# Two-block transformer layer stack on one core: in the RWKV pairs, the last accumulator's scaling, the output gate's product and the rounding of the output change places

## The reference, cut to what matters

```python
r, k, v, wd, ad, gd = _split(z, RWKV_SIZES)
decay = jnp.exp(-jnp.exp(w_log)); a = jax.nn.sigmoid(a0 + ad @ a2)
g = jax.nn.sigmoid(gd) @ g2                      # the output gate
def step(S, inp):                                # a scan over 512 tokens
    Sa = einsum('bhvk,bhk->bhv', S, a_t)
    S = S * w_t + Sa * b_t + v_t * k_t
    return S, einsum('bhvk,bhk->bhv', S, r_t)
y = (y - mu) * rsqrt(var + RWKV_LN_EPS) * lnx_g + lnx_b
y = (y + bonus) * g                              # -> y @ w_rwkv_o
```

## Time and profile before

| | us |
|---|---|
| runs shown | 2666.18, 2668.07, 2661.59; median 2666.18 |
| the profiled execution, its own time | 2665.71 |
| its span, first to last instruction | 2663.9 |
| granted TensorE clock, mean | 0.994 of full speed |
| PE busy | 2592.7 (97% of the span) |
| DVE busy | 1457.7 (55%) |
| ACT busy | 632.8 (24%) |
| POOL busy | 1485.9 (56%) |

### The profile page before, as it was taken

The page is one execution under the profiler, slowest core; times in us unless marked ns, Lnnn a source line. Parts: engine busy times, 40 slices in busy tenths (PEclk is TensorE's granted clock), DMA queues, the critical chain, the costliest instruction groups (busy, mean ns, idle before and its releaser), DMA issues.

```text
span 2663.9 us, 47379 instructions
## 1 busy us (share of the span) xinstructions
PE 2592.7 (97%) x16370; PEld 2024.5 (76%) x16370; DVE 1457.7 (55%) x2041; ACT 632.8 (24%) x1159; POOL 1485.9 (56%) x945
## 2 busy tenths in 40 slices
PE   7889999998999999999999999999999999999999
PEld 5667888876776677777888887776677777888887
DVE  7886646364566647774442424557647764443434
ACT  3332000023234414431200002234423431200002
POOL 4466666655544544556666666554444456666665
PEclk9999999999999999999999999999999999999999
DMA  4213233323211122223333333311122223233322
GB/s 152 68 44 103 88 95 93 95 84 103 87 57 50 42 93 60 78 71 97 92 95 94 95 95 108 96 57 42 50 85 68 76 72 100 90 95 94 95 94 95
DMA packets 72725, 222.67 MB, mean 84 GB/s; under 512 B 9344, under 2 KB 12544, under 8 KB 72576
## 3 DMA queue, kind: packets, MB, share of 16 engines
q1 hardware_dynamic: 72576, 220.63, 27.1%
HBM read 218.50 MB, written 2.10 MB: 83 GB/s over the span
## 4 chain that ended last, share of the span: by engine, by line
PE 89%; DVE 5%; DVEq 3%; issue 1%; DMA 1%; POOL 1%; ACT 0%; SPq 0%; ACTq 0%; POOLq 0%
PE acc L479 78%; PE bank L479 10%; DMA raw<-in_w_pg 1%; POOL w_lo L358 0%; PE bank L1057 0%; DVE z L1095 0%; DVEq L1538 0%; DVE rw_bon L1095 0%; DVEq L1275 0%; DVEq L1631 0%; DVE rw_SCB L1095 0%; DVE z_rw L1095 0%; DVE att L1293 0%; DVEq L1294 0%; DVEq L1286 0%
## 5 line engine op out<-in xcount | busy, mean ns | idle before, releaser
L358 POOL TENSOR_TENSOR w_lo<-raw,w_hi 128x1024 fp32r<-128x1024 f32 (+3 forms) x438 | 964.0, 2201 | 298.8 <-PE acc L479 277.9
L351 POOL TENSOR_SCALAR w_hi<-raw 128x1024 fp32r<-128x1024 f32 (+3 forms) x438 | 431.5, 985 | 689.2 <-PE acc L479 585.1
L479 PE MATMUL acc<-xg_hi,w_hi 128*128 128x512 f32 x2224 | 594.9, 404 | 26.8 <-POOL w_lo L358 12.6
L479 PE MATMUL acc<-xg_hi,w_lo 128*128 128x512 f32 x2224 | 587.7, 399 | 0.0
L479 PE MATMUL acc<-xg_lo,w_hi 128*128 128x512 f32 x2224 | 585.7, 399 | 0.0
L479 PEld LDWEIGHTS acc<-xg_hi,w_hi 128*128 128x128 f32 x2224 | 412.3, 189 | 145.8 <-issue 52.3
L479 PEld LDWEIGHTS acc<-xg_lo,w_hi 128*128 128x128 f32 x2224 | 416.9, 189 | 103.7 <-issue 4.8
L479 PEld LDWEIGHTS acc<-xg_hi,w_lo 128*128 128x128 f32 x2224 | 415.0, 188 | 100.0
L1095 DVE TENSOR_TENSOR x<-x,acc 128x512 f32<-128x512 f32 x104 | 71.4, 688 | 322.3 <-PE acc L479 322.0
L1910 ACT ACTIVATE ffn_act<-ffn_t 128x512 f32<-128x512 f32 x100 | 63.3, 633 | 775.7 <-DVEq L1155 619.5
L479 PE MATMUL acc<-hid_hi,w_hi 128*128 128x512 f32 x656 | 182.8, 396 | 3.8 <-POOL w_lo L358 1.6
(11 more groups left out here) (339 smaller groups left out, 2795.1 us busy)
## 6 DMA issues: line engine op xcount, KB each, us to landing
raw<-in_w_up SPq DMA_DIRECT2D x132, 512.0 KB, 3.6
raw<-in_w_down SPq DMA_DIRECT2D x48, 512.0 KB, 3.6
raw<-in_w_gate SPq DMA_DIRECT2D x48, 512.0 KB, 3.6
raw<-in_w_ret SPq DMA_DIRECT2D x32, 512.0 KB, 3.6
raw<-in_w_rw SPq DMA_DIRECT2D x28, 512.0 KB, 3.6
raw<-in_w_o SPq DMA_DIRECT2D x48, 256.0 KB, 2.6
raw<-in_w_in SPq DMA_DIRECT2D x18, 512.0 KB, 3.7
raw<-in_w_down SPq DMA_DIRECT2D x24, 384.0 KB, 3.0
```

The source lines that it names most:

```text
L351: nc.gpsimd.tensor_scalar(w_hi[:, s, 0:n], raw[:, s, 0:n], 1.0, 0.0, ALU.mult, ALU.add).then_inc(w_half[s], 1)
L358: nc.gpsimd.tensor_tensor(w_lo[:, s, 0:n], raw[:, s, 0:n], bits(w_hi[:, s, 0:n]), ALU.subtract).then_inc(w_split[s], 1)
L479: return nc.tensor.matmul(o, a, b, start=first, stop=last, skip_group_check=shared)
```

## The change

Five edits, all in the RWKV pairs:

- DVE: the last `take(1, 1)` of pair j becomes `last_take(j)` and moves, for j < 3, from the end of the pair's state steps into the next pair, behind `say("ops")`. For j = 3 it stays.
- The output gate's product leaves `variance` (and `bank[2]`) and becomes `output_gate(j-1)` into `bank[5]`, issued by PE in the first fill of level 4 of pair j, with 2 passes instead of 5. DVE's `gated` is split: the two `scalar_tensor_tensor` stay behind `ops` (`scaled_output`), the product with the gate (`gate_output`) moves to level 5. For pair 3 both stay together behind the pairs.
- PE's wait for `gd` moves from the transposes in the head to a place behind the `dd` products.
- DVE: `high(j-1)` moves from level 3 to behind state step 2, `low(j-1)` from level 4 to behind state step 4.
- PE's passes are dealt out anew: 9 instead of 7 ahead of `kh` (j > 0), 2 (1 for j = 3) new ones ahead of the `y0` products, 1 (2 for j = 0) instead of 3 (2 for j = 3) behind them. There are 96 in a pair before and after.

```diff
@@ -770,7 +770,9 @@
                 def variance(j):
                     after("ysq", j, 1, 1)
                     head_sums(bank[3][:], rw["Lr"][:]).then_inc(s2["yvar"], 1)
-                    mm(bank[2][:], K["g2"][:, j, :], z_rw[:, 13, :], True, True).then_inc(s2["gate"], 1)
+
+                def output_gate(j):
+                    mm(bank[5][:], K["g2"][:, j, :], z_rw[:, 13, :], True, True).then_inc(s2["gate"], 1)
 
                 def rwkv_pair(j):
 
@@ -789,7 +791,7 @@
                     fill(14)
                     if j > 0:
                         variance(j - 1)
-                    fill(7)
+                    fill(7 if j == 0 else 9)
                     after("kh", j, 1, 1)
                     for n in range(NT):
                         mm(bank[0][:, n * P:(n + 1) * P], z_rw[:, 8 + j, n * P:(n + 1) * P], rw["centre"][:], True, True)
@@ -813,8 +815,6 @@
                             last = mm(bank[(5, 0)[p]][half[c], n * P:(n + 1) * P], rw["kp"][half[p], chunk(n, c)],
                                       rw["AR"][half[p], n, :, half[c]], True, True)
                     last.then_inc(s2["sc"], 1)
-                    if j > 0:
-                        after("gd", j - 1, 1, 1)
                     for n in range(NT):
                         last = nc.tensor.transpose(bank[2][:, n * P:(n + 1) * P], rw["AR"][:, n, 0, :], K["ident"][:])
                     last.then_inc(s2["tr"], 1)
@@ -843,6 +843,13 @@
                             fill(4)
                             after("wev", j, 1, 1)
                             lora(j + 1)
+                        elif lev == 4 and j > 0:
+                            if j < 3:
+                                after("sig", j + 1, 1, 1)
+                            else:
+                                after("wev", j, 1, 1)
+                            output_gate(j - 1)
+                            fill(2)
                         else:
                             fill(5)
                         after("gev", j, 2 * lev - 1, 11)
@@ -876,6 +883,9 @@
                             last = mm(bank[2 + c][half[p], col(n)], rw["tokK"][half[c], n, half[p]], rw["tokV"][half[c], n, half[p]],
                                       False, True, True)
                     last.then_inc(s2["dd"], 1)
+                    fill(2 if j < 3 else 1)
+                    if j > 0:
+                        after("gd", j - 1, 1, 1)
                     for n in range(NT):
                         for p, c in both:
                             mm(bank[4 + c][half[p], col(n)], AU[half[c], p, n, 1, :], SCB[half[c], p, n, 1, :], n == 0, False, True)
@@ -884,7 +894,7 @@
                             last = mm(bank[4 + c][half[p], col(n)], rw["tokV"][half[c], n, half[p]], SCK[half[c], p, n, 1, :],
                                       False, False, True)
                     last.then_inc(s2["y0"], 1)
-                    fill(3 if j < 3 else 2)
+                    fill(2 if j == 0 else 1)
                     after("qev", j, 1, 1)
                     after("y0", j, 1, 1)
                     for i in range(1, 2 * NT):
@@ -946,6 +956,7 @@
                 slot(0, I, xg, full)
                 slot(1, I, xg, full)
                 variance(3)
+                output_gate(3)
                 slot(0, I + 1, xg, full)
                 slot(1, I + 1, xg, full)
                 query_sums(0)
@@ -1570,6 +1581,11 @@
 
                 def gated(j):
 
+                    scaled_output(j)
+                    gate_output(j)
+
+                def scaled_output(j):
+
                     zk = z_rw[:, 4 + j, :]
                     after("yroot", j, 1, 1)
                     dve.sem_inc(dve_turn, 1)
@@ -1577,8 +1593,12 @@
                     dve.drain()
                     v.scalar_tensor_tensor(zk, zk, pcol(V_LNB + j, 1), z_rw[:, j, :], ALU.add, ALU.add)
                     dve.drain()
+
+                def gate_output(j):
+
+                    zk = z_rw[:, 4 + j, :]
                     after("gate", j, 1, 1)
-                    tt(zk, zk, bank[2][:])
+                    tt(zk, zk, bank[5][:])
                     say("gd")
 
                 def high(j):
@@ -1613,6 +1633,9 @@
                     tt(kk, kk, bank[0][:])
                     say("kh")
 
+                def last_take(j):
+                    scaled(1, I + 2 * j + 1, z_rt[:, 4 * j + 3, :]).then_inc(acc_free[1], 1)
+
                 def rwkv_pair(j):
 
                     F = I + 2 * j
@@ -1633,7 +1656,8 @@
                     tt(eM, ra, eM)
                     say("ops")
                     if j > 0:
-                        gated(j - 1)
+                        last_take(j - 1)
+                        scaled_output(j - 1)
 
                     after("sc", j, 1, 2)
                     for p in range(2):
@@ -1661,9 +1685,9 @@
                             key_scores(0)
                         elif lev == 2:
                             take(1, 0)
-                        elif lev == 4 and j > 0:
-                            low(j - 1)
                         elif lev == 5:
+                            if j > 0:
+                                gate_output(j - 1)
                             take(0, 1)
                             if j < 3:
                                 decays(j + 1, 1)
@@ -1675,8 +1699,6 @@
                             say("xt", 2)
                         if lev == 1:
                             key_scores(1)
-                        elif lev == 3 and j > 0:
-                            high(j - 1)
                         elif lev == 4 and j < 3:
                             decays(j + 1, 4)
                     after("au", j, 1, 1)
@@ -1700,11 +1722,15 @@
                         v.scalar_tensor_tensor(rw["S"][:, i + 1, :], rw["S"][:, i, :], rw["pc"][:, n, c:c + 1],
                                                bank[2 + c][:, n * HD:(n + 1) * HD], ALU.mult, ALU.add)
                         say("st")
+                        if j > 0 and i == 2:
+                            high(j - 1)
+                        elif j > 0 and i == 4:
+                            low(j - 1)
                     if j < 3:
                         norms(j + 1)
-                    if j == 3:
+                    else:
                         after("tl", j, 6, 6)
-                    take(1, 1)
+                        last_take(j)
 
                 rw_order = (12, 13, 0, 4, 8, 1, 5, 9, 2, 6, 10, 3, 7, 11)
                 for i in range(RW_PAIRS):
```

## The result

The changed kernel takes 2678.66 us in the median of 7 runs (2675.06 to 2681.81); the kernel before, in 7 runs, 2668.07 us (2661.59 to 2668.97). The ratio is 1.0045, with a 95% interval of 1.0035 to 1.0054: 0.45% slower, some 12 us (the two medians lie 10.6 us apart). The profiled execution has a span of 2676.9 us, against 2663.9 us before: 13.0 us more.

The account below looks back on a forecast made before the run. PE, busy 97% of the span, was taken as the bound. Terms 4.2 (head) + 0 (gate) + 0.2 (split passes) + 8.2 (rounding) = +12.6 us on the 2666.2 median gave 2678.8 us; 8 in 10: 2668 to 2688.

Parts of the forecast that it names:

- Removing the scaling ahead of `keys_hat` is worth nothing: End of the state steps: removing 0.69 us of DVE gains 0, as DVE waits for ACT's exponential and `rw_bon` starts unchanged.
- The 25th pass waits for `ops` plus the scaling, 1.6 us: Pair's head: PE waits 1.6 us, the old 0.93 goes; net +0.7 a pair, +4.2 us over six.
- The gate product and its reader, 0: Level 4's first fill and level 5: moving PE's gate product and DVE's product with the gate costs 0.
- Passes split in two, +0.2: Fill ahead of `y0`: extra shape changes cost 0.7 us, one pass more in pair 3 gives -0.25 twice; together +0.2 us.
- Rounding in the state steps, +8.2: State steps: POOL's weight splits block DVE's cast and subtraction, making states late; +8.2 us, ends 0.6 and 12.6.
- the 1.34 worked out: State steps of pair 1: the state update behind the blocked subtraction comes 1.34 us late.
- the 1 us or more that the forecast gave as a sign: State steps: the cast `y_hi<-z_rw` at 1 us or more would show the forecast right.
- The worst phase, 2.1 us in pair 2: Pair 2, first layer: the cast falls just behind the start of a `w_lo`, making the state 2.1 us late.

Follow-up runs that it names:

- experiment three: Changed kernel with the last accumulator's scaling back at the end of the state steps, all else kept: 2668.56 us, ratio 1.0008 to the kernel before.
- Experiment four: Kernel before with only the passes behind the `y0` products split, 2 (1 in pair 3) going ahead of them: 2665.20 us, ratio 0.9994.
- experiment two: Kernel before with only `high` and `low` moved from levels 3 and 4 to behind state steps 2 and 4: 2683.55 us, ratio 1.0065.
- experiment seven: Changed kernel with 7 passes ahead of `kh` and 16 behind the transposes, the 25th behind the scores: 2674.92 us, ratio 1.0025 to the kernel before.

## Why the prediction was right, and which of its terms were not

The forecast of 2678.8 us and the measured 2678.66 agree better than their terms do. That the kernel gets slower by some 10 us, at the 25th pass and in the state steps, was worked out; that the sum is right to 0.2 us is luck.

- **Removing the scaling ahead of `keys_hat` is worth nothing**: right. `rw_bon` starts with the exponential in both kernels, and experiment three puts the scaling back without cost.
- **The 25th pass waits for `ops` plus the scaling, 1.6 us**: right, 1.51 to 1.52 in all six pairs; also that POOL's `w_hi` comes earlier without the gate product ahead of PE's 16th pass and so leaves `rw_a` alone (0.68 us), and that level 1 stops waiting. The term was 0.7 a pair, the rows give 1.51 - 0.93 = 0.6. Undoing the move gave more than these 3.5 us, for two reasons: with the scaling in front the rest of the change leaves only 0.27 of the old 0.93 us, so the move itself costs 6 x 1.24 = 7.4 us and the rest of the change gives 4 us back at the head; and in the trace of experiment three the clock fell once less.
- **The gate product and its reader, 0**: no wait for `gd`, `gate` or ahead of the `au` products is seen in the changed kernel.
- **Passes split in two, +0.2**: wrong in sign. The shape changes were priced; that the split would also end the unnamed stalls was not seen. They fell by 3.7 us. Experiment four shows that the split does it: with it alone they fall by 3.4 us. The theory, that a run of some 160 small products outpaces the delivery of instructions, fits this, but no row shows a delivery: the cause of the stalls stays open.
- **Rounding in the state steps, +8.2**: the mechanism right, the size too big. The added waits on the states sum to 5.2 us (6.7 us of waits less the 1.5 that pair 3 had before, 0.49 and 0.28 in each layer). In pair 1 the states are 1.28 us late against the 1.34 worked out, but PE waits for only 1.08 us of that, as it has products to lay in. The cast itself took 0.43 to 0.81 us, not the 1 us or more that the forecast gave as a sign; the subtraction carried the part, 1.15 to 1.19. The worst phase, 2.1 us in pair 2, did not come in the changed kernel. There an unnamed stall of 0.91 us had stood ahead of the state steps, and it is 0.18 us now, so the cast comes ahead of the split. Where a longer one was left the phase came: experiments two (stalls of 1.18 and 0.92 us, waits of 1.71 and 1.95) and seven (0.45 and 0.47, waits of 2.08 and 2.04).
- **The clock** has no term in the forecast. From the stretch behind pair 3 it is (12.85 - 11.30) + (13.55 - 11.30) = 3.8 us, and 0.4 inside pair 3 of the second layer, where that pair is 44.68 us long and its twin in the first layer 44.23. This is the step that was missing: the sum stopped at PE's waits and took PE's rate as given.

Together the measured terms are 3.5 (head) + 5.2 (states) + 4.2 (clock) - 3.1 (unnamed stalls, 3.7 less the 0.6 that the states' term has already) = 9.8 us of the 13.2 in the pairs. The other 3.4 stay open; up to 1.4 of them are the 0.17 us for each extra change of shape in 8 pairs, and waits of under 0.2 us don't show in the profile. Two errors, a missed loss and a missed gain, and one term too large have cancelled.

The Trainium skill ("SBUF — State Buffer", "Who interferes with whom") says that DVE and GpSimd share a port pair which the first to issue holds for its whole instruction, and that a DVE instruction with at most one SBUF input outside the 2-port modes takes no part. Traces agree with both: 2.55 us for a cast that starts 0.08 us behind a split and 0.43 for one that starts 0.20 us ahead of it (the split then takes 2.44 us instead of 2.35), and 0.692 us for either operation fed from PSUM, whatever POOL does.

## What to carry to other kernels

Before an operation is moved into an engine's waiting time, look at what the neighbour on the shared port does in that very stretch: its price there is its duration and also the rest of the neighbour's instruction. Before a release (here of an accumulator) is moved back, count the instructions up to the first one that needs it; the 25th pass, one place ahead of the scores, turned a free move into a wait of 1.5 us a pair. And where an engine is the bound, a sum over its waits is not the whole bill, since longer waits can also lower the rate at which it works afterwards.

## What the runs showed of the hardware that was not expected

- TensorE's granted clock fell to 0.50 behind pair 3 although no single wait there was above 1.02 us. PE worked on small 64x64 products with one pass between them, waited 0.59 and 1.01 us, and then ran its full-size passes at 1.2 GHz: eight in 3.27 us instead of 1.97. Such waits don't always do it: of the four traces with rounding in pair 3 out of SBUF, those of the changed kernel (waits of 0.59 and 1.01 us) and of experiment two (0.79 and less) had it in both layers, those of experiments three and seven (as in the changed kernel) in the first layer alone. The six other traces, the largest wait on a state of pair 3 being 0.51 us, had it in neither. So waits of this size are needed for it at this place, and they don't suffice. Another place has it as well: inside pair 2 the clock fell in both layers of experiment seven, behind waits of 2.08 and 2.04 us, and in neither layer of experiment two, behind 1.71 and 1.95.
- Unnamed stalls of 0.5 to 1.6 us among 160 small products in a row (in the kernel before and in experiment two) are gone or at most 0.48 us long in the eight kernels in which one or two full-size passes stand in the middle.
